# Rolling the mixer passes of a decoder trunk into loops on all five queues

## The reference, cut to what matters

```python
def token_mixer(x, ...):                      # x: 256 tokens x 1024
    proj = x @ w_in                           # q/k/v of 3 attention groups, retention q, k, v, g, two gates
    # 3 dilated windows, 8 heads of 128, softmax; 4 retention heads, keys 256, values 512
    attn = (weights * jnp.stack(outs, 0)).sum(0)
    ret = silu(ret_g) * head_group_norm(chunkwise_retention(...))
    merged = sigmoid(gate_a) * (attn @ w_attn_proj) + sigmoid(gate_r) * (ret @ w_ret_proj)
    return merged @ w_out

for i in range(2):
    x = layer_norm(ALPHA * x + token_mixer(x, ...))
    ple = sigmoid(x @ w_ple_gate[i]) * (p[i] @ w_ple_proj[i])
    x = layer_norm(ALPHA * x + conv_ffn(x, w_up[i], ...) + ple)
```

## Time and profile before

| what | value |
|---|---|
| median of 3 runs | 1550.85 us (1550.83 to 1550.88) |
| the profiled execution | 1550.83 us, span 1549.0 us, mean granted TensorE clock 0.999 |
| TensorE, VectorE, ScalarE, GpSimd busy | 99%, 59%, 48%, 1% of the span |
| matmuls | 11770, with as many weight loads |
| read from memory | 263.50 MB |

### The profile page before, as it was taken

One profiled execution on the slowest core, in us unless ns is written; L12 is line 12 of the kernel. 1 busy time (PEld: TensorE's weight loads), 2 busy tenths in 40 slices (PEclk: granted clock), 3 DMA queues, 4 the chain that ended last, 5 costly groups with the idle time before them and its releaser, 6 DMA issues.

```text
span 1549.0 us, 27139 instructions
## 1 busy us (share of the span) xinstructions
PE 1530.7 (99%) x11770; PEld 1482.6 (96%) x11770; DVE 919.6 (59%) x1001; ACT 744.1 (48%) x783; POOL 22.9 (1%) x23
## 2 busy tenths in 40 slices
PE   8999999999999999999999999999999999999998
PEld 7999999999999989999999999999999999899997
DVE  5564554745544486666865636556455445676677
ACT  5454454444533345556544544535445333465553
POOL 0000000000000010000000000000000000100000
PEclk9999999999999999999999999999999999999999
DMA  8544535445446565556444545454553564655551
GB/s 285 187 136 163 181 119 190 137 163 164 163 156 202 173 205 175 201 178 217 164 163 163 164 159 163 138 177 134 164 183 117 183 217 150 218 190 184 179 198 63
DMA packets 231483, 265.93 MB, mean 172 GB/s; under 512 B 4192, under 2 KB 221792, under 8 KB 230880
## 3 DMA queue, kind: packets, MB, share of 16 engines
q1 hardware_dynamic: 231248, 264.44, 51.4%
q10 hardware_dynamic: 144, 0.13, 0.0%
HBM read 263.50 MB, written 1.05 MB: 171 GB/s over the span
## 4 chain that ended last, share of the span: by engine, by line
PE 93%; DVE 4%; ACT 1%; DMA 1%; issue 1%; SPq 0%; DVEq 0%
PE bank L1013 26%; PE bank L1014 26%; PE bank L1015 26%; PE acc L1013 3%; PE acc L1014 3%; PE acc L1015 3%; PE acc L1103 1%; DVE w_lo L596 1%; PE acc L1121 1%; PE acc L1130 1%; DMA raw<-w_in 1%; PE acc L1118 1%; PE acc L1105 1%; DVE stat L618 1%; ACT w_hi L358 0%
## 5 line engine op out<-in xcount | busy, mean ns | idle before, releaser
L596 DVE TENSOR_TENSOR w_lo<-raw,w_hi 128x2048 fp32r<-128x2048 f32 x241 | 551.7, 2291 | 447.0 <-ACT w_hi L358 446.7
L1013 PE MATMUL bank<-xT_hi,w_hi 128*128 128x256 f32 x2240 | 637.2, 284 | 0.0
L1015 PE MATMUL bank<-xT_hi,w_lo 128*128 128x256 f32 x2240 | 633.8, 283 | 0.0
L1014 PE MATMUL bank<-xT_lo,w_hi 128*128 128x256 f32 x2240 | 633.8, 283 | 0.0
L358 ACT ACTIVATE w_hi<-raw 128x2048 fp32r<-128x2048 f32 x243 | 463.9, 1911 | 158.6 <-PE bank L1015 98.3
L1013 PEld LDWEIGHTS bank<-xT_hi,w_hi 128*128 128x128 f32 x2240 | 429.8, 192 | 1.9 <-DVE w_lo L596 0.4
L1014 PEld LDWEIGHTS bank<-xT_lo,w_hi 128*128 128x128 f32 x2240 | 429.8, 192 | 1.6
L1015 PEld LDWEIGHTS bank<-xT_hi,w_lo 128*128 128x128 f32 x2240 | 429.8, 192 | 0.0
L1013 PE MATMUL bank<-w_hi,xT_hi 128*128 128x256 f32 x768 | 219.5, 286 | 3.8 <-DVE w_lo L596 2.0
L1015 PE MATMUL bank<-w_hi,xT_lo 128*128 128x256 f32 x768 | 217.2, 283 | 0.0
L1014 PE MATMUL bank<-w_lo,xT_hi 128*128 128x256 f32 x768 | 217.2, 283 | 0.0
(11 more groups left out here) (156 smaller groups left out, 1450.9 us busy)
## 6 DMA issues: line engine op xcount, KB each, us to landing
raw<-w_in SPq DMA_DIRECT2D x135, 1024.0 KB, 5.0
raw<-w_up SPq DMA_DIRECT2D x44, 1024.0 KB, 5.0
raw<-w_down SPq DMA_DIRECT2D x20, 1024.0 KB, 4.8
raw<-w_ret_proj SPq DMA_DIRECT2D x16, 1024.0 KB, 4.9
raw<-w_attn_proj SPq DMA_DIRECT2D x8, 1024.0 KB, 5.0
raw<-w_out SPq DMA_DIRECT2D x8, 1024.0 KB, 4.8
raw<-w_ple_gate SPq DMA_DIRECT2D x8, 1024.0 KB, 4.9
scratch<-ln_rows SPq DMA_DIRECT2D x4, 1024.0 KB, 6.9
```

The costliest lines, as they stand in the source:

```text
L596: nc.vector.tensor_tensor(w_lo[:, s, :], raw[:, s, :], w_hi[:, s, :].bitcast(F32), ALU.subtract).then_inc(lo_ready, 1)
L1013: mm(dst, st_hi, mv_hi, start=start, stop=False)
L1014: mm(dst, st_hi, mv_lo, start=False, stop=False)
L1015: return mm(dst, st_lo, mv_hi, start=False, stop=stop)
```

## The change

On each queue, the Python loop over j = 1, 2, 3, which wrote three copies of the pass, becomes a hardware loop with one copy. j is then a register in these passes, and so are all thresholds, the column offsets of the weight loads, and the places in `attn_hi`, `ret_hi`, `feat` and `decay` that depend on j. Pass 0 remains written out; the test that picks it out becomes `isinstance(j, int)`.

```diff
-                for j in range(1, NJ):
-                    mixer_loads(l, L0 + j * C_MIX, j, 0)
+                with sp.Fori(1, NJ) as j:
+                    mixer_loads(l, sp.snap(L0 + j * C_MIX), j, 0)
...
-                first = j == 0
+                first = isinstance(j, int)
...
-                for j in range(1, NJ):
+                with act.Fori(1, NJ) as j:
                     mixer(l, j)
...
-                for j in range(1, NJ):
+                with dve.Fori(1, NJ) as j:
                     mixer(l, j)
...
-                for j in range(1, NJ):
+                with pool.Fori(1, NJ) as j:
                     group_rstd(l, j)
...
-                for j in range(1, NJ):
+                with pe.Fori(1, NJ) as j:
                     mixer(l, j)
```

## The result

The changed kernel takes 1559.92 us (median of 4 runs, 1558.87 to 1561.86) against 1550.84 us, a ratio of 1.006 (95% interval 1.0043 to 1.0078). It is slower by 9.1 us. The forecast was 1552.1 with a range up to 1558. The first rival has come true: TensorE's code is not there at the jump back. The span of the profiled execution is 1558.9 us, 9.9 more than the 1549.0 before.

The account below looks back on a forecast made before the run. TensorE alone was taken to bound the mixer. Zero for all jumps back plus 1.2 us for register thresholds, on 1550.85, gave 1552.1 us; the 8-in-10 range was 1550.6 to 1558.

Parts of the forecast that it names:

- The first rival: TensorE's code is missing at the four mixer jumps back: 1554 to 1558 us, dearer if wholly uncovered; chance 0.22.
- (a): TensorE's four jumps back between mixer passes 1 to 3 cost 0 us, as in the merge loop.
- (c): Register thresholds delay VectorE's chain to TensorE's line 1130 at two places: 0.20 us per pass, 1.2 us over six.
- (b): Jumps back on VectorE, ScalarE, GpSimd and SyncE cost 0 us, hidden by 10.7 us of cover.
- the cover at chunk 2: At a mixer pass's start, VectorE's w_lo is done 10.7 us before TensorE reaches that chunk, hiding stalls up to 6.6.
- The row of ScalarE: ScalarE's line 524 follows TensorE equally in the MLP loop and its constant copy, 16.98 us apart: registers cost nothing there.
- rival 2: All six links of the chain, or the pass start too, pay for registers: 4.3 us or more, 1555 up; chance 0.08.
- the chain: VectorE and ScalarE work from chunk 9's end to tile 0's probabilities: ready 286.81, used by TensorE 286.94, practically no room.
- The list of rooms: Room of every TensorE wait in a mixer pass: all but tile 0's probabilities have 4 us or more.
- The list of waits: What TensorE waited for in the profile: said to hold nothing of the mixer, longest the load of x at the start.

Follow-up runs that it names:

- slot 160: Changed kernel without a hint, head of TensorE's loop placed at place 160 of a 256-instruction fetch block: 1558.89 us, ratio 1.0054.
- slots 0 and 96: Two runs of the changed kernel without a hint, TensorE's loop head at place 0 or 96 of a 256-instruction fetch block: 1550.72 and 1550.82 us.
- slots 200: Changed kernel without a hint, head of TensorE's loop at place 200 of a 256-instruction fetch block: 1563.03 us, ratio 1.0077.
- slot 239: Changed kernel without a hint, head of TensorE's loop at place 239 of a 256-instruction fetch block: 1579.39 us, ratio 1.0182.

## Why the prediction was wrong

**The step that failed is (a)**, "The jump, with the register sums and the first wait behind it, costs TensorE 0.0 us ... I take 0 for the four." It measured 1.76, 2.30, 1.91 and 3.70 us. I took the price of the merge loop, whose 536 matmuls and loads span about two blocks, for a pass that spans more than six. That row showed what a jump costs to code that is held, and nothing about what is held. The evidence on size was in the text, as the first rival, with a chance of 0.22. Its sum was sound: 0.5 to 1.5 us per jump gave 1554 to 1558, and 2.1 us gave 1560.5. The measured 1.8 to 2.3 us per jump, with a fall of the clock after some, lie at its upper price, and I had put the range below that. That 1560.5 lies so near to 1559.92 is in part luck: it holds 1.2 us of (c), which measured nothing, and lacks the fall of the clock.

**What stands in its place.** The pass of the changed kernel ran past what TensorE holds, by some 20 instructions (an estimate from its nearness to slot 160, below). Passes that end in the 7th block from their head jump back free and are not fetched again (1360 instructions, or 1650 at slots 0 and 96). The same 1650 instructions, ending in the 8th, lose their head. Where the head of the changed kernel lay can be read from the transfers: the last one before its branch starts 0.9 to 1.1 us before it over the four jumps, which is near slot 160 (0.7 to 1.4) and far from slots 200 (3.2 to 3.9) and 239 (5.1 to 5.5). Its four holes and its 86 blocks are those of slot 160 too. That eight blocks are held, one of them fetched ahead, is the reading that fits all the runs and the times of the transfers: a pass that touches eight fetches nine at each jump, its own and the one behind, and a pass that touches seven fetches none. How the hint holds back the block behind the pass is not shown.

The Trainium skill, "Runtime: NRT & Kernel Launch", section on instruction fetch mechanics, gives TensorE 2048 instructions in blocks of 256, which is eight blocks. The runs agree with the size, and with the sentence that a taken branch out of the window stalls the engine. They don't agree with the same section where it makes this window two pages of 16 KiB: a pass of seven blocks is jumped over free. Nor do they agree that full unrolling is the remedy: held or hinted loops cost nothing (1550.69 to 1550.82 us). The Trainium skill, "Advanced Engine Details and Errata", Engine Queue Depths, gave me an estimate of 3.9 us of cover, by which the jumps would have been nearly free; this trace shows 2.1 us of work in hand when the branch starts (208.1 to 210.20), and holes of 1.5 to 2.0 us.

**(b) was right.** VectorE, ScalarE, GpSimd and SyncE cost nothing with their loops (1550.83 us), and the cover at chunk 2 was still 10.7 us.

**(c) was wrong**, though it made no difference to the outcome. The 0.20 us per pass measured 0.00: VectorE starts 0.03 us after the end of TensorE's matmul. I had carried over the 0.12 us of line 889, a line that computes the address of an operand, to lines that only compare a threshold. The row of ScalarE that I used against rival 2, where a register cost nothing, was the nearer one. That the chain has practically no room stays untested, as nothing lengthened it. The list of rooms missed one below 4 us: VectorE ends the rotated rows at 281.88 + 0.42 = 282.30 and TensorE uses them from line 1177 at 285.64, 3.3 us later. The list of waits has one entry of the mixer too, 0.5 us at 19.44 in the first pass. Neither changes the sum.

**What I had not priced** is the clock. A hole of about 2 us was followed by 1.2 GHz for 3.4 us after one of four jumps in one profile and after two of four in another, and after none at slots 160 and 200; at slot 239 it was at that level for 6.8 us at each of the four. With 1.7 us each this would account for most of the spread: the four runs of the changed kernel lie 3 us apart, those of before beside them 0.2, and over all its runs 1.0. It is read from one profile of each kernel and not shown for the other runs. Why the clock falls after one such hole and not after the next is open.

## What to carry to other kernels

Before rolling a long body into a loop, count the instructions per engine and ask whether head and end are held together, and read the duration of the branch in the trace; the free jump of a shorter loop in the same trace is no evidence. Here TensorE's limit lay between an end in the 7th and one in the 8th block of 256 instructions from the head, so that code placed ahead of the loop can shift the body across it. A hint for the jump back, a fixed slot for the head or a short inner loop each took the loss away, and none made the kernel faster than the written-out one, whose code was fetched in time all along.

## What the runs showed of the hardware

- A lost head held TensorE's queue at the branch for 3.3 to 3.9 us, against 0.2 to 0.3 us for a taken branch whose code was held and 0.08 us for one not taken. TensorE had 2.1 us of work in hand, and stood for 1.5 to 2.0 us. The whole pass was fetched again: 86 blocks against 50, nine per jump.
- The transfer of the block after the head's started 4.4 to 4.9 us after the head's, so that a head near the end of its block cost a second hole: 3.2 to 3.6 us with 17 instructions in it, 0.7 to 0.9 us with 56, and none with 96 (slot 160).
- After the holes of slot 239 the granted clock was 0.50, the 1.2 GHz level, in the first 2 us of work behind the second one too (216 to 218). In that profile the span is 30.2 us longer than before (1579.2), where the holes add up to 13.4 + 6.4 = 19.8. Some 4 us of work per jump at half the clock, 2 us lost each, are about 8 of the rest (an estimate).
- Thresholds in registers cost nothing that could be measured on any of the five queues (1550.83 us with them on four, 1550.69 on all five, against 1550.85).
